# Index scores that trail their query tiles by two in a hybrid decoder step on one core

## Chip, cores and metric

One core of a Trainium2 chip runs the whole kernel. The metric is device time in microseconds (us) of one execution; the number given for a version is the median of its runs.

## What is computed

One inference step of a decoder layer, for a prompt of 256 tokens with 16 meta tokens ahead (272 rows) and for 8 samples with a paged cache of 1,024 tokens each (8 more rows, 280 in all). What matters here is how the attention picks its keys:

```python
proj = jnp.einsum('btd,dc->btc', _rmsnorm(x, g_mix_pre), w_in)
q, k, v, iq, ik, iw, u = jnp.split(proj, IN_OFFSETS, axis=-1)
s = jnp.einsum('bqhd,bsd->bqsh', iq, ik).astype(jnp.float32) * (IDX_DIM ** -0.5)
w = iw.astype(jnp.float32) * (N_IDX_HEADS ** -0.5)
scores = jnp.einsum('bqsh,bqh->bqs', jax.nn.relu(s), w)      # 16 index heads of width 64
_, idx = lax.top_k(jnp.where(admissible, scores, -jnp.inf), topk)
# attention over the chosen keys; pooling mixer on u; output projection; gated FFN with a short convolution
```

## The kernel before

Everything is float32, computed as three matmuls per product: a weight chunk is split into `hi` (ACT copies it, L415) and `lo` (DVE subtracts, L423), and PE multiplies hi by hi, hi by lo and lo by hi (L1409, L1410, L1412). A chunk is 128 x 1024 weights, 512 KB; SP loads it into one of four `raw` slots (L453) once the `lo` of the chunk four before is done. Two chunks make one tile of 128 output columns: 48 matmuls. The chunks are numbered in the order of the program: `C_IK` 0 and 1, `C_IQ` from 2 (eight index query tiles), `C_PROJ` from 18 (twenty tiles: eight of u, two each of k and v, eight of q), then the output projection `C_WOP`, `C_WOA`, the FFN.

Each engine has its program written out by hand, runs it in order and waits on semaphores. Around the change:

- PE: `q_idx_tile(0, t)` makes index query tile t, which holds index heads 2t and 2t+1; `weights_turned` (L1474) turns the heads' weights and lets DVE go on (`iw_ready`); `index_scores(h, p)` (L1470) multiplies the queries of heads h and h+1 with the index keys into banks 2 and 4. After the tiles come the scores of the last 16 queries (`iq3`, L1516), their weighted sum (L1521), then `proj_tile` by `proj_tile`, with the sample scores (L1540) after the first and their sum (L1548, waits for `sum3_used`) after the second.
- ACT: the `hi` of the chunks, the relu of each head's scores (`relu_head`, L668), and once, at the start, `root(1)` (L649, L652), the inverse root of the RMSNorm, with two loads of function tables.
- DVE: the `lo` of the chunks; `inv_rms(1)`; the index keys; `index_queries(t)` (seven instructions, the last is L896), which scales the queries of tile t; `index_sum(h)` (L954), which adds head h to the scores S; later, between projection tiles, nine `prompt_round` (top 8 of each row), `sample_lists`, `prompt_mask`, sixteen `sort_round` and `merge_lists`. In the attention loop over eight heads it does, for head h+1, `masked_scores` (L1177), then one piece of the sample's selection (`merge_quarters`, `compare_quarters`, `sample_threshold`, `sample_mask_1` to `3`), then the `lo` of a chunk, `head_low` (L1187) and the scaling of the probabilities (L1194, L1197), on which PE's transposes for the head wait (L1639).
- SP: between the weight loads it copies 64 cache pages, two DMAs each (`pages`, L464 to L466): three pages after an index tile's two chunks, then four, then two.

A head of the attention loop on PE is: transposes of the probabilities, scores of the next head (L1586), in heads 1, 2, 4 and 5 the `sample_scores` (L1597), the values (L1658 to L1660), one half tile of the output projection (24 matmuls).

## Time and profile before

| what | value |
|---|---|
| runs | 1218.87, 1219.74, 1219.9 us; median 1219.74 |
| the profiled execution | 1220.88 us, of which 1219.1 us are the span of the trace |
| PE busy | 1165.0 us (96%) |
| DVE busy | 816.8 us (67%) |
| ACT busy | 541.1 us (44%) |
| mean granted TensorE clock | 0.979 of full speed |
| DMA | 238.76 MB, mean 196 GB/s |

The trace has the start and duration of every instruction, and for an engine's idle time the event that ended it, in square brackets.
### The profile page before, as it was taken

The page shows a single profiled execution, that of the slowest core. Times are in us where ns is not written, and L with a number is a line of the kernel's source. Part 1 is how long each engine was busy: PE and PEld are TensorE (multiplying, and loading weights), DVE is VectorE, ACT ScalarE, POOL GpSimd, SP SyncE. Part 2 cuts the span into 40 slices and gives each one's busy share as a digit, 9 for nine tenths or more (in the row PEclk, how much of TensorE's full clock was granted, in tenths as well). Part 3 has the DMA queues.
Part 4 walks back from the last instruction along what each step waited for, and adds up shares of the span by engine and source line. Part 5 has one row for each costly group of instructions (what it writes and reads, how often), then busy time and mean ns, then how long its engine had stood idle before and what let it go on. Part 6 is the DMA issues. An engine that isn't in the chain of part 4 may idle for free.

```text
span 1219.1 us, 25889 instructions
## 1 busy us (share of the span) xinstructions
PE 1165.0 (96%) x9165; PEld 1120.7 (92%) x9165; DVE 816.8 (67%) x1543; ACT 541.1 (44%) x769; POOL 63.9 (5%) x70
## 2 busy tenths in 40 slices
PE   8989999999899899999999999999999899999992
PEld 7879999767698699999999999999999899999992
DVE  4775798776357977777777777777776444444444
ACT  7343333333235755445455544545454243333431
POOL 4700000000000400000000000000000000000002
PEclk9999999899899999999999999999999999999997
DMA  8878879655864365555555555555556666666641
GB/s 304 319 247 262 252 240 310 213 189 175 275 239 155 108 202 184 165 188 171 187 167 180 176 169 187 170 187 167 183 175 196 207 177 180 181 177 186 177 138 71
DMA packets 81080, 238.76 MB, mean 196 GB/s; under 512 B 9440, under 2 KB 28992, under 8 KB 78704
## 3 DMA queue, kind: packets, MB, share of 16 engines
q1 hardware_dynamic: 75152, 225.40, 57.9%
q10 hardware_dynamic: 4480, 9.01, 2.1%
q0 software_dynamic: 1408, 3.84, 0.9%
q8 instruction: 23, 0.38, 0.1%
q14 instruction: 17, 0.14, 0.0%
HBM read 231.64 MB, written 24.16 MB: 210 GB/s over the span
## 4 chain that ended last, share of the span: by engine, by line
PE 85%; DVE 6%; DMA 3%; SPq 3%; issue 1%; ACT 1%; DVEq 0%; POOL 0%; ACTq 0%; POOLq 0%
PE bank L1409 27%; PE bank L1410 27%; PE bank L1412 27%; DMA raw<-in_w_in 1%; DMA cache_ring<-vscr 1%; DVE part L1281 1%; DVE lo L423 1%; DMA x<-xscr 1%; PE bank L1586 1%; PE bank L1621 1%; SPq L466 1%; SPq L465 1%; SPq L464 0%; DVE h_lo L1286 0%; DVE short L1177 0%
## 5 line engine op out<-in xcount | busy, mean ns | idle before, releaser
L1409 PE MATMUL bank<-h_hi,hi 128*128 128x266 f32 (+1 forms) x2096 | 605.7, 289 | 1.5 <-DVE lo L423 1.5
L1412 PE MATMUL bank<-h_hi,lo 128*128 128x266 f32 (+1 forms) x2096 | 604.4, 288 | 0.0
L1410 PE MATMUL bank<-h_lo,hi 128*128 128x266 f32 (+1 forms) x2096 | 603.5, 288 | 0.0
L423 DVE TENSOR_TENSOR lo<-raw,hi 128x1024 fp32r<-128x1024 f32 (+2 forms) x362 | 431.5, 1199 | 212.9 <-ACT hi L415 189.9
L415 ACT ACTIVATE hi<-raw 128x1024 fp32r<-128x1024 f32 (+2 forms) x362 | 373.6, 1034 | 310.2 <-PE bank L1412 287.4
L1409 PEld LDWEIGHTS bank<-h_hi,hi 128*128 128x128 f32 x2096 | 399.0, 190 | 6.6 <-issue 4.4
L1410 PEld LDWEIGHTS bank<-h_lo,hi 128*128 128x128 f32 x2096 | 397.5, 190 | 0.1
L1412 PEld LDWEIGHTS bank<-h_hi,lo 128*128 128x128 f32 x2096 | 397.1, 189 | 0.0
L1409 PE MATMUL bank<-g_hi,hi 128*128 128x264 f32 x704 | 200.3, 285 | 5.0 <-DVE lo L423 5.0
L1410 PE MATMUL bank<-g_lo,hi 128*128 128x264 f32 x704 | 201.2, 286 | 0.0
L1412 PE MATMUL bank<-g_hi,lo 128*128 128x264 f32 x704 | 200.3, 284 | 0.0
L1409 PEld LDWEIGHTS bank<-g_hi,hi 128*128 128x128 f32 x704 | 133.4, 190 | 5.3 <-DVE lo L423 5.3
L1412 PEld LDWEIGHTS bank<-g_hi,lo 128*128 128x128 f32 x704 | 133.2, 189 | 0.0
L1410 PEld LDWEIGHTS bank<-g_lo,hi 128*128 128x128 f32 x704 | 132.8, 189 | 0.0
L1314 DVE SCALAR_TENSOR_TENSOR act<-up,par,act 128x256 f32<-128x256 f32 x176 | 84.9, 482 | 12.3 <-DVE act L1314 0.2
L807 ACT ACTIVATE g_hi<-act 128x264 f32 (+1 forms) x44 | 18.7, 425 | 143.4 <-DVE act L1328 143.4
L800 ACT ACTIVATE act<-up,par 128x264 f32<-128x264 f32 x88 | 53.5, 608 | 23.7 <-DVE up L1303 23.7
L432 POOL TENSOR_TENSOR o<-o,rms 128x528 f32<-128x528 f32 (+1 forms) x2 | 4.4, 2200 | 787.9 <-DVE rms L910 787.9
L821 ACT ACTIVATE act<-act 128x264 f32<-128x264 f32 x44 | 18.7, 425 | 50.3 <-DVE act L1317 50.3
L1330 DVE TENSOR_TENSOR g_lo<-act,g_hi 128x264 f32 (+1 forms) x44 | 19.1, 434 | 31.0 <-ACT g_hi L807 31.0
L1303 DVE TENSOR_TENSOR up<-bank,rms 128x266 f32<-128x266 f32 x88 | 37.6, 428 | 0.1
L599 POOL DMA_INDIRECT cache_ring<-in_cache_kidx,kix x32 | 34.0, 1064 | 23.2 <-DVE kix L875 13.8
(256 smaller groups left out, 651.0 us busy)
## 6 DMA issues: line engine op xcount, KB each, us to landing
raw<-in_w_up SPq DMA_DIRECT2D x176, 512.0 KB, 3.6
raw<-in_w_in SPq DMA_DIRECT2D x56, 512.0 KB, 5.2
raw<-in_w_down SPq DMA_DIRECT2D x64, 448.0 KB, 3.4
raw<-in_w_o SPq DMA_DIRECT2D x32, 512.0 KB, 4.5
raw<-in_w_down SPq DMA_DIRECT2D x32, 512.0 KB, 3.6
kscr<-in_cache_k SPq DMA_DIRECT2D x64, 128.0 KB
vscr<-in_cache_v SPq DMA_DIRECT2D x64, 128.0 KB
mixed<-kscr SPq DMA_DIRECT2D x8, 512.0 KB, 7.0
```

What stands on the lines that cost most here:

```text
L415: nc.scalar.activation(hi[:, s, 0:width], raw[:, s, 0:width], ACT.Copy).then_inc(hi_ready, 1)
L423: ops.tensor_tensor(lo[:, s, 0:width], raw[:, s, 0:width], hi[:, s, 0:width].bitcast(F32), ALU.subtract).then_inc(done, 1)
L599: nc.gpsimd.indirect_dma_start(kidx[:, b, g * PAGE:(g + 1) * PAGE], None, kidx_rows, bass.IndirectOffsetOnAxis(ap=kix[:, n:n + 1], axis=0) ...
L800: nc.scalar.activation(act[:, v, :], up[:, p, v, CONV - 1:], ACT.Identity, scale=par[:, bass.ds(CWT + 4 * FT + f, 1)], bias=par[:, bass.ds ...
L807: nc.scalar.activation(g_hi[:, bass.ds(r, 1), :], act[:, 0:1, :], ACT.Copy).then_inc(g_hi_ready, 1)
L821: nc.scalar.activation(act[:, 0, :], act[:, 0, :], ACT.Silu).then_inc(silu_ready, 1)
L1303: nc.vector.tensor_tensor(up[:, p, v, :], bank[(T_UP + v) % 2][:, L:T], rms[:, L:], mul).then_inc(up_ready, 1)
L1314: st.link(nc.vector.scalar_tensor_tensor(act[:, v, 0:SEQ], up[:, p, v, i:i + SEQ], par[:, bass.ds(CWT + 2 * FT * i + f, 1)], act[:, v, 0:S ...
L1330: nc.vector.tensor_tensor(g_lo[:, bass.ds(r, 1), :], act[:, 0:1, :], g_hi[:, bass.ds(r, 1), :].bitcast(F32), ALU.subtract).then_inc(g_lo_r ...
L1409: mm(out, w_hi, x_hi[:, k, first:], start=(opens and done == 0), stop=False)
L1410: mm(out, w_hi, x_lo[:, k, first:], start=False, stop=False)
L1412: last = mm(out, w_lo, x_hi[:, k, first:], start=False, stop=(closes and done == total))
```

## The change

Four index query tiles are kept instead of two (`iq`), and tile 3 gets a bank of its own. PE makes tiles 2 and 3 before `weights_turned` and the first scores; from there on the scores of tile t-2 follow tile t. Scores of the last heads (14) and of the last queries, the weighted sum and the sample scores move behind the projection tiles 0, 1 and 2. ACT and DVE split chunks `C_IQ + 6` and `C_IQ + 7` earlier, one of them ahead of `root(1)`; the relus and index sums lag accordingly. On DVE two rounds of the prompt's selection move into the q tiles, the sixteen sort rounds stand in the last three q tiles instead of four, and `merge_lists` and every later piece of the sample's selection move one place on, so that the attention loop starts with `merge_lists` and its head 6 has `sample_mask_3`.

```diff
@@ -244,7 +244,7 @@
-    iq = short[:, 0:2 * T].rearrange("p (h t) -> p h t", h=2)
+    iq = short[:, 0:4 * T].rearrange("p (h t) -> p h t", h=4)
@@ -288,7 +288,7 @@
-        return bank[3 if t == 2 else (T_IQ + t) % 2]
+        return bank[(3, 5)[t - 2] if t in (2, 3) else (T_IQ + t) % 2]
@@ -651,9 +651,10 @@
-            hi_chunk(ae, 0, C_IQ + 4)
-            hi_chunk(ae, 0, C_IQ + 5)
+            for j in range(4, 7):
+                hi_chunk(ae, 0, C_IQ + j)
...
+            hi_chunk(ae, 0, C_IQ + 7)
@@ -669,31 +670,25 @@
-            for t in (1, 2):
-                if t > 1:
-                    hi_chunk(ae, 0, C_IQ + 2 * t + 2)
-                    hi_chunk(ae, 0, C_IQ + 2 * t + 3)
-                for p in range(2):
-                    relu_head(2 * (t - 1) + p, p)
-            with ae.Fori(1, 3) as i:
-                for t in (1, 2):
-                    hi_chunk(ae, i, C_IQ + 2 * t + 2)
-                    hi_chunk(ae, i, C_IQ + 2 * t + 3)
-                    for p in range(2):
-                        relu_head(4 * i + 2 * (t - 1) + p, p)
-            hi_chunk(ae, 0, C_PROJ)
-            hi_chunk(ae, 0, C_PROJ + 1)
-            for h in range(12, 16):
+            def hi_tile(cj):
...
+                hi_chunk(ae, 0, cj)
+                hi_chunk(ae, 0, cj + 1)
...
+            for t in range(4, 9):
+                hi_tile(C_IQ + 2 * t)
+                for n in range(0 if t == 4 else 2 * t - 8, 2 * t - 6):
+                    relu_head(n, n % 2)
+            for h in range(10, 14):
...
-                if h < 14:
-                    hi_chunk(ae, 0, C_PROJ + h - 10)
-                if h == 13:
-                    ae.wait_ge(score3_done, 1)
-                    for n in range(2):
-                        nc.scalar.activation(relu3[n], bank[3 + 2 * n][:, 0:TP], ACT.Relu,
-                                             scale=IDX_SCALE).then_inc(relu3_ready, 1)
-            hi_chunk(ae, 0, C_PROJ + 4)
-            hi_chunk(ae, 0, C_PROJ + 5)
+            hi_tile(C_PROJ + 2)
+            for h in range(14, 16):
+                relu_head(h, h % 2)
+            ae.wait_ge(score3_done, 1)
+            for n in range(2):
+                nc.scalar.activation(relu3[n], bank[3 + 2 * n][:, 0:TP], ACT.Relu,
+                                     scale=IDX_SCALE).then_inc(relu3_ready, 1)
+            hi_tile(C_PROJ + 4)
@@ -881,8 +876,8 @@
-                if t >= 2:
-                    dve.wait_ge(iq_used, 2 * t - 2)
+                if t >= 4:
+                    dve.wait_ge(iq_used, 2 * t - 6)
@@ -893,7 +888,7 @@
-                nc.vector.tensor_tensor(iq[:, t % 2, L:], ps[:, L:T], rms[:, L:], mul).then_inc(iq_ready, 1)
+                nc.vector.tensor_tensor(iq[:, t % 4, L:], ps[:, L:T], rms[:, L:], mul).then_inc(iq_ready, 1)
@@ -920,7 +915,9 @@
+            lo_chunk(dve, nc.vector, lo_dve, 0, C_IQ + 6)
...
+            lo_chunk(dve, nc.vector, lo_dve, 0, C_IQ + 7)
@@ -961,23 +958,20 @@
-                if t in range(2, 8):
+                if t >= 3:
...
-                if t >= 2:
-                    index_sum(2 * t - 4)
-                    index_sum(2 * t - 3)
+                    index_sum(2 * t - 6)
+                    index_sum(2 * t - 5)
...
-            for h in range(12, 16):
-                index_sum(h)
-                if h == 13:
-                    lo_chunk(dve, nc.vector, lo_dve, 0, C_PROJ + 2)
-                    lo_chunk(dve, nc.vector, lo_dve, 0, C_PROJ + 3)
-            dve.wait_ge(sum3_done, 1)
-            acc = S[0:16, S_AT[2]:S_AT[2] + TP]
-            nc.vector.tensor_tensor(acc, acc, misc[0:16, 128:128 + TP], ALU.add).then_inc(sum3_used, 1)
-            dve.wait_ge(sum3_used, 1)
...
+            def index_sum_3():
...
+                dve.wait_ge(sum3_done, 1)
+                acc = S[0:16, S_AT[2]:S_AT[2] + TP]
+                nc.vector.tensor_tensor(acc, acc, misc[0:16, 128:128 + TP], ALU.add).then_inc(sum3_used, 1)
+                dve.wait_ge(sum3_used, 1)
@@ -1075,11 +1069,18 @@
                     lo_chunk(dve, nc.vector, lo_dve, 0, C_PROJ + 2 * t + j)
 
             for t in range(U0, U0 + 8):
-                if t:
-                    low_halves(t + 1)
+                if t == 0:
+                    index_sum(10)
+                    index_sum(11)
+                low_halves(t + 1)
+                if t < 2:
+                    index_sum(2 * t + 12)
+                    index_sum(2 * t + 13)
                 if t == 2:
+                    index_sum_3()
+                if t == 3:
                     sample_lists()
-                else:
+                elif t >= 2:
                     prompt_round(next(rounds_p))
                 ps = tile_ready(t)
                 nc.vector.tensor_tensor(U[:, t, POOL_BUF:POOL_BUF + T], ps[:, 0:T], rms[:, :],
@@ -1131,15 +1132,13 @@
                 h = t - Q0
                 if h < HEADS - 1:
                     low_halves(t + 1)
-                if h < 2:
+                if h < 4:
                     prompt_round(next(rounds_p))
-                if h == 2:
+                if h == 4:
                     prompt_mask()
-                if h in range(3, 7):
-                    for n in range(4 * h - 12, 4 * h - 8):
+                if h >= 5:
+                    for n in range(((0, 5, 10, 16))[h - 5], ((0, 5, 10, 16))[h - 4]):
                         sort_round(n)
-                if h == 7:
-                    merge_lists()
                 ps = tile_ready(t)
                 g = h // (HEADS // KV)
                 off = 32 * g + h
@@ -1200,17 +1199,19 @@
                 if h + 1 < HEADS:
                     masked_scores(h + 1)
                     if h == 0:
+                        merge_lists()
+                    if h == 1:
                         merge_quarters()
                         compare_quarters(0, 4)
-                    if h == 1:
+                    if h == 2:
                         compare_quarters(4, 8)
-                    if h == 2:
+                    if h == 3:
                         sample_threshold()
-                    if h == 3:
+                    if h == 4:
                         sample_mask_1()
-                    if h == 4:
+                    if h == 5:
                         sample_mask_2()
-                    if h == 5:
+                    if h == 6:
                         sample_mask_3()
                     lo_chunk(dve, nc.vector, lo_dve, 0, C_WOP + 4 + h)
                     head_low(h)
@@ -1459,15 +1460,16 @@
-            def index_scores(h, p):
...
-                if not isinstance(h, int) or h >= 2:
+            def index_scores(h):
...
+                pe.wait_ge(iq_ready, h // 2 + 1)
+                if h >= 2:
...
-                        last = mm(o, iq[rows, p, q0:q0 + nq], ikT[rows, 0:nk], start=True, stop=True)
+                        last = mm(o, iq[rows, h // 2 % 4, q0:q0 + nq], ikT[rows, 0:nk], start=True, stop=True)
@@ -1500,26 +1495,15 @@
+            q_idx_tile(0, 3)
...
-            for t in range(2):
-                pe.wait_ge(iq_ready, t + 1)
-                index_scores(2 * t, t)
-            with pe.Fori(1, 3) as i:
-                q_idx_pair(i, i)
-            pe.wait_ge(iq_ready, 6)
-            q_idx_tile(0, 7)
-            pe.wait_ge(iq_ready, 7)
-            index_scores(12, 0)
...
-            pe.wait_ge(iq_ready, 8)
-            for n in range(2):
-                last = mm(bank[3 + 2 * n][:, 0:TP], iq3[:, P * n:P * n + P], ikT[0:IDX_DIM, 0:TP], start=True, stop=True)
-            last.then_inc(score3_done, 1)
-            index_scores(14, 1)
-            pe.wait_ge(relu3_ready, 2)
-            for n in range(2):
-                last = mm(misc[0:16, 128:128 + TP], iwq3[:, n, :], relu3[n], start=(n == 0), stop=(n == 1))
-            last.then_inc(sum3_done, 1)
+            index_scores(0)
+            index_scores(2)
+            for t in range(4, 8):
+                pe.wait_ge(iq_ready, t - 3 if t < 6 else t - 1)
+                q_idx_tile(0, t)
+                index_scores(2 * t - 4)
+            index_scores(12)
@@ -1530,6 +1514,15 @@
+            index_scores(14)
+            for n in range(2):
+                last = mm(bank[3 + 2 * n][:, 0:TP], iq3[:, P * n:P * n + P], ikT[0:IDX_DIM, 0:TP], start=True, stop=True)
+            last.then_inc(score3_done, 1)
+            proj_tile(0, 1, T_PROJ + 1)
+            pe.wait_ge(relu3_ready, 2)
+            for n in range(2):
+                last = mm(misc[0:16, 128:128 + TP], iwq3[:, n, :], relu3[n], start=(n == 0), stop=(n == 1))
+            last.then_inc(sum3_done, 1)
@@ -1540,14 +1533,15 @@
-            proj_tile(0, 1, T_PROJ + 1)
+            proj_tile(0, 2, T_PROJ + 2)
...
-            with pe.Fori(0, 5) as i:
+            proj_tile(0, 3, T_PROJ + 3)
+            with pe.Fori(1, 5) as i:
```

On ACT, at the start of the program (`rms` is the inverse root, `hi` a chunk's high half), before and after:

```order
L415 ACTIVATE hi<-raw 128x1024 [waits chunk_used,raw_loaded2]
L415 ACTIVATE hi<-raw 128x1024 [waits chunk_used,raw_loaded3]
L649 ACT_TABLE_LOAD
L649 ACTIVATE rms<-bank,con 128x280 [waits sum_ready]
L652 ACT_TABLE_LOAD
L652 ACTIVATE rms<-rms 128x280 [waits ln_ready]
L658 DMA part<-in_pool_w 128x2048 [waits h_lo_ready]
L659 DMA part<-in_state_pool 128x960
L668 ACTIVATE short<-bank 128x384 [waits iq_used] x2
```

```order
L415 ACTIVATE hi<-raw 128x1024 [waits chunk_used,raw_loaded2]
L415 ACTIVATE hi<-raw 128x1024 [waits chunk_used,raw_loaded3]
L415 ACTIVATE hi<-raw 128x1024 [waits chunk_used,raw_loaded0]
L649 ACT_TABLE_LOAD
L649 ACTIVATE rms<-bank,con 128x280 [waits sum_ready]
L652 ACT_TABLE_LOAD
L652 ACTIVATE rms<-rms 128x280 [waits ln_ready]
L415 ACTIVATE hi<-raw 128x1024 [waits chunk_used,raw_loaded1]
L659 DMA part<-in_pool_w 128x2048 [waits h_lo_ready]
L660 DMA part<-in_state_pool 128x960
L415 ACTIVATE hi<-raw 128x1024 [waits chunk_used,raw_loaded2]
L415 ACTIVATE hi<-raw 128x1024 [waits chunk_used,raw_loaded3]
```

The high half of `C_IQ + 6` now stands ahead of the table loads, with its wait for the chunk's DMA, and three more high halves ahead of the first relus.

On DVE, after the weights of the index heads are there (`iwq`, `iwz`; L886 to L891 are one `index_queries`), the order is now:

```order
L939 COPY iwq<-bank 128x32 [waits iw_ready,iq_ready]
L941 TENSOR_TENSOR iwq<-bank,con 128x16 x2
L943 TENSOR_TENSOR iwz<-bank,con 128x8
L886 TENSOR_TENSOR short<-bank,rms 64x4 [waits chunk_used,s_loaded,dve_step]
...
L891 TENSOR_TENSOR short<-bank,rms 128x266
L886 TENSOR_TENSOR short<-bank,rms 64x4 [waits chunk_used,iq_ready]
...
L891 TENSOR_TENSOR short<-bank,rms 128x266
L423 TENSOR_TENSOR lo<-raw,hi 128x1024 [waits chunk_used,hi_ready,iq_ready]
L423 TENSOR_TENSOR lo<-raw,hi 128x1024 [waits chunk_used,hi_ready]
```

Before, one `index_queries` stood between `iwq` and the first `lo` (that of `C_IQ + 6`); now two stand there, and the first `lo` is that of `C_IQ + 8`.

On DVE, in head 6 of the attention loop (L1176 and L1180 are the end of `masked_scores`, L1196 the scaling that PE waits for):

```order
L1180 TENSOR_SCALAR nmx<-mx 128x2 [waits dve_step]
L1181 TENSOR_SCALAR nmx<-mx 16x1
L1056 SCALAR_TENSOR_TENSOR short<-Ss,thr,short 8x1025
L1057 TENSOR_TENSOR Ws<-Ws,short 8x1025 [waits dve_step]
L1058 TENSOR_SCALAR Ws<-Ws 8x1025 [waits dve_step]
L423 TENSOR_TENSOR lo<-raw,hi 128x1024 [waits chunk_used,hi_ready]
L1186 TENSOR_TENSOR h_lo<-bank,h_hi 128x258 [waits o_hi]
L1193 RECIPROCAL rden<-den 128x3 [waits exp_done]
L1196 TENSOR_SCALAR short<-short,rden 128x128 [waits dve_step]
```

Before, head 6 had nothing between its `masked_scores` and the `lo`; these three instructions of `sample_mask_3` stood in head 5.

## Rows read from the trace of the kernel before

**Rows 1.** Stretches of the index stage and the projections: busy time by engine, clock, DMA

```profile
core 0: us, PE busy (x) PEld busy (x) DVE busy (x) ACT busy (x) POOL busy (x), PEclk, DMA share, GB/s
27.40:32.60 5.20, 5.20 (x42) 5.11 (x42) 2.81 (x3) 5.15 (x6) 4.18 (x4) 1.00 0.92 278
39.65:44.68 5.03, 2.74 (x25) 1.92 (x25) 3.13 (x13) 2.76 (x4) 3.97 (x4) 1.00 1.03 407
44.68:52.33 7.65, 7.65 (x49) 7.50 (x49) 7.32 (x18) 2.88 (x4) 6.02 (x6) 0.78 0.83 275
52.33:59.31 6.98, 6.98 (x57) 6.50 (x56) 5.72 (x15) 2.77 (x4) 5.26 (x6) 1.00 0.78 249
80.27:88.88 8.61, 5.20 (x26) 2.21 (x25) 6.34 (x17) 4.21 (x8) 0.00 (x0) 0.83 0.71 235
88.88:96.97 8.09, 8.09 (x49) 7.93 (x48) 3.63 (x13) 1.06 (x1) 0.00 (x0) 0.76 0.72 232
96.97:113.50 16.53, 16.53 (x140) 15.16 (x140) 9.49 (x27) 5.38 (x7) 0.00 (x0) 1.00 0.77 242
107.24:217.35 110.11, 110.11 (x872) 110.03 (x873) 91.41 (x242) 37.15 (x38) 0.00 (x0) 1.00 0.84 271
```

**Rows 2.** Timeline of PE: the small products of the index stage

```profile
52.33 0.93 PE L1470 MATMUL bank<-ikT,short 64*128 64x128 f32 x8
82.75 1.18 PE L1516 MATMUL bank<-ikT,short 64*128 64x272 f32 x4 [1.56 <-DVE short L896]
86.89 1.99 PE L1521 MATMUL bank<-short,iwq 128*16 128x272 f32 x4 [0.41 <-ACT short L693]
```

**Rows 3.** Timeline of DVE behind the turned weights

```profile
40.71 0.19 DVE L942 COPY iwq<-bank 128x32 f32<-128x32 f32 x1 [2.11 <-PE bank L1482]
41.17 0.35 DVE L891 TENSOR_TENSOR short<-bank,rms 64x4 f32<-64x4 f32 x2
42.35 0.43 DVE L896 TENSOR_TENSOR short<-bank,rms 128x266 f32<-128x266 f32 x1
43.40 2.36 DVE L423 TENSOR_TENSOR lo<-raw,hi 128x1024 fp32r<-128x1024 f32 x2 [0.61 <-DVE short L896]
```

**Rows 4.** Weight loads of chunks C_IQ + 6 and + 7, from issue to landing

```profile
L453 SPq DMA_DIRECT2D raw<-in_w_in x2: 430/501/572, 27.4 to 28.0; - x2
...
DMA to landing us min/median/max: 5.2/5.2/5.2
```

**Rows 5.** Timeline of ACT, the inverse root

```profile
29.58 1.28 ACT L649 ACT_TABLE_LOAD   x1
30.88 0.49 ACT L649 ACTIVATE rms<-bank,con 128x280 f32<-128x280 f32 x1
32.69 0.44 ACT L652 ACTIVATE rms<-rms 128x280 f32<-128x280 f32 x1
```

**Rows 6.** Timeline of SP's queue, the loads of query tile 6 and projection tile 3

```profile
53.96 0.94 SPq L453 DMA_DIRECT2D raw<-in_w_in  x2
...
97.90 0.95 SPq L453 DMA_DIRECT2D raw<-in_w_in  x2
```

**Rows 7.** Heads 0, 1, 3, 4, 5, 6 of attention, transposes to transposes (columns of rows 1)

```profile
230.95:240.88 9.93, 9.83 (x43) 7.54 (x43) 6.94 (x27) 3.27 (x11) 0.00 (x0) 0.66 0.27 99
240.88:249.22 8.34, 8.34 (x58) 5.78 (x59) 5.94 (x23) 3.48 (x10) 0.00 (x0) 1.00 0.23 71
257.54:266.36 8.82, 6.75 (x44) 5.18 (x43) 6.65 (x19) 4.32 (x11) 0.00 (x0) 1.00 0.92 296
266.36:277.03 10.67, 10.03 (x58) 6.42 (x59) 7.04 (x18) 2.98 (x10) 0.00 (x0) 0.84 0.78 246
277.03:286.37 9.34, 8.51 (x59) 5.74 (x59) 7.10 (x19) 3.69 (x11) 0.00 (x0) 1.00 0.17 59
286.37:293.33 6.96, 6.80 (x42) 5.23 (x43) 4.09 (x16) 2.70 (x11) 0.00 (x0) 1.00 0.32 96
```

**Rows 8.** DVE from start to end of each selection piece: merge_lists, merge_quarters, threshold, masks 1 to 3

```profile
212.29:216.67 4.38, 4.10 (x17) 1.00 1.01 332
235.13:238.33 3.20, 2.96 (x11) 0.50 0.00 0
252.84:254.73 1.89, 1.69 (x8) 1.00 0.00 0
261.14:263.82 2.68, 2.61 (x6) 1.00 1.10 361
271.40:274.49 3.09, 3.02 (x5) 1.00 0.98 332
280.69:283.85 3.16, 3.09 (x6) 1.00 0.00 0
```

More of the change, by code:

```diff
@@ L1482, in weights_turned @@
                 mm(misc[:, 64:72], con[0:16, HREP:HREP + P], iwT[:, TP:T], start=True, stop=True).then_inc(iw_ready, 1)
-            def q_idx_pair(r, n):
-                for t in (1, 2):
-                    pe.wait_ge(iq_ready, 2 * n + t - 1)
-                    q_idx_tile(r, t)
-                    pe.wait_ge(iq_ready, 2 * n + t)
-                    index_scores(4 * n + 2 * (t - 1), (t - 1) % 2)
             ident = con[:, IDN:IDN + P]
```

## The prediction

> **What bounds the kernel now.** I read the busy times first, then a table of stretches with the granted clock, then PE's timeline with the event that ended each pause. PE is busy 96% of the span and DVE 67%, so only time that PE loses, or spends at its lower clock, counts. From 107.24 to 217.35 us PE is busy for 110.11 of 110.11 us at clock 1.00, that is 2.4 GHz: nothing can be won there [rows 1]. It loses time in three places.
>
> The first is the pause before index tile 3: in 5.03 us PE works 2.74, so 2.29 are lost, and the tile behind it takes 7.65 at a mean clock of 0.78 [rows 1]. The next stretch, one tile and one product of scores, takes 6.98 at clock 1.00; without the scores (0.93, [rows 2]) a tile is 6.05, so the fall of the clock cost 1.6. The second is the end of the index stage: 8.61 us with 5.20 busy, so 3.41 lost, and the projection tile behind it takes 8.09 at clock 0.76 [rows 1], against about 6.2 at full clock (16.53 us hold two tiles and the sample's products): 1.9. PE's last product there stretched to 1.99, at half clock [rows 2]. The third is attention, where the intervals are longer than PE's busy time in heads 0, 3, 4 and 5 [rows 7].
>
> **The index stage, to the start of projection tile 3.** Before, it starts at 113.50 [rows 1]. After, tile 2 still ends at about 39.65 and tile 3 follows at once, so to 45.7, if its weights are there. Its chunks land at 27.4 + 5.2 = 32.6 and little later [rows 4]. The high half of C_IQ + 6 now stands ahead of root(1) on ACT and waits for that landing: root(1), which began at 29.58 and took 3.55 to 33.13 [rows 5], begins near 33.6 and moves 4 us back, to about 37.2. The index keys and queries 0 behind it on DVE, and the split of C_IQ + 7, then end near 40 to 42; PE needs the split inside tile 3, at about 42.7 (half of the tile), and the queries at 46. So I cost the move at nothing; its cover is tile 3, and 1 us more would eat most of it.
>
> Then the weights are turned. From the end of tile 2 (39.65, [rows 1]) to DVE's copy of them took 1.06, to 40.71; from there to the end of queries 1 it took 2.07, to 42.78 [rows 3]. After: copy at 46.8, queries 1 at 48.8. PE does scores 0 meanwhile and is done at 47.6, so it idles 1.2; scores 2 end at 49.8. But now a second set of queries (1.6, from 41.17 to 42.78) stands on DVE ahead of the first low half that tile 4 needs (1.2; two took 2.36): 48.8 + 1.6 + 1.2 = 51.6 [rows 3]. PE idles 1.8 more. **The first pause is not removed; it moves behind tile 3 and becomes 3.0 instead of 2.29.** With the same fall of the clock behind it (1.6), tile 4 ends at 51.6 + 6.05 + 1.6 = 59.3. Before, it ended at 59.31, with one product of scores more done.
>
> From there on: scores 4 (0.93), tiles 5 to 7 with scores (3 x 6.98 = 20.95), about 1.0 of waiting for two relus of ACT before scores 12 (one wait of that kind took 0.41, [rows 2]; two relus on ACT are more; between 0.4 and 2), scores 12 (0.93), three projection tiles with the sample's products (16.53 + 6.2 = 22.73, [rows 1]), scores 14 (0.93), the last queries (1.18, [rows 2]) and their weighted sum (1.99 at half clock, so 1.0): 49.65. Tile 3 of the projection starts at 109.0 instead of 113.50: **4.5 us gained**. The waits of the second pause now lie beside projection tiles.
>
> SP is the next to be late. It may load a chunk once the low half of the chunk four before is done. The loads of tile 6 wait for the low half of C_IQ + 9, at 52.8, so they leave 1.1 earlier than 53.96 [rows 6], and since SP's queue is full of page copies behind them, so do later loads: those of projection tile 3 at 96.8 instead of 97.90 [rows 6], while PE is 4.5 ahead. Landing takes 5.2 [rows 4], the two high halves and the last low half about 3, the sum of the last queries, which stands behind them on DVE and on which PE's sample sum waits, about 0.5: 105.7. PE gets there at 109.0 less half of the 4.1 that the sample's two products take (16.53 - 2 x 6.2), about 106.9. About 1.2 us of slack: hidden, but a gain over 5.7 is cut off here.
>
> **The projections.** A moved index sum, prompt round or sort round delays PE only if DVE falls behind by more than the two banks allow. DVE is busy 91.41 of 110.11 us [rows 1], and the last three query tiles get five or six sort rounds instead of four. Cost nothing; the cover is that DVE's slack.
>
> **Attention.** A head's interval is the longer of PE's own path and DVE's, on which PE's transposes wait. DVE's path is a fixed part plus that head's selection piece: head 3 has 8.82 with a piece of 2.68, so 6.14 fixed [rows 7, 8]; head 5, 9.34 - 3.16 = 6.18, agrees. PE's own path is 8.34 with sample scores (heads 1, 2, 4, 5) and about 6.8 without (head 6, 6.80 busy) [rows 7]. Each piece moves one head on, and merge_lists (4.38, [rows 8]), which was hidden under a projection tile, joins head 0:
>
> - head 0: 9.93 - 3.20 + 4.38 = 11.11
> - head 1: 6.14 + 3.20 = 9.34 (was 8.34)
> - head 2: 8.34; its piece fitted into 8.34 in head 1
> - head 3: 6.14 + 1.89 = 8.03 (was 8.82)
> - head 4: 6.14 + 2.68 = 8.82 (was 10.67)
> - head 5: 6.14 + 3.09 = 9.23 (was 9.34)
> - head 6: 6.14 + 3.16 = 9.30 (was 6.96)
>
> That is 64.17 against 62.38 (286.37 + 6.96 - 230.95): 1.8 lost. In it head 4's 10.67 is gone: by the rule it was 9.23, and 1.44 came from half clock after the 2.07 of idle in head 3 (8.82 - 6.75) [rows 7]. After, that pause shrinks to 1.3, but head 6 idles 9.30 - 6.80 = 2.5, and I price the fall behind it at the same 1.44: **3.2 us lost**. Masks 2 and 3, which fell into heads with 8.34 of PE work, now fall partly into heads without.
>
> **Sum.** -4.5 + 3.2 = -1.3: the profiled execution goes from 1220.88 to 1219.5. It lies 1.14 above the median of 1219.74, so the median becomes 1218.4. Bounds: index stage -5.7 (SP's limit) to -2.6 (one more fall of 1.9), attention +1.8 to +6 (three falls): from -3.9 to +3.4.
>
> **The rivals.** *Faster:* the clock recovers inside the pause of tile 4, which PE's short products at 47 and 49 break in two, so tile 4 runs at full speed; the index stage then gains up to SP's limit, 5.7, and if head 6's pause costs no fall either, attention loses 1.8: -3.9, 1215.8. For it: the two idle pieces are 1.2 and 1.8, each shorter than head 3's 2.07, after which the clock fell. Against: the pause of 2.29 before tile 3 was broken by small products as well, and tile 3 ran at 0.78. *Slower:* falls also follow the new short pauses, before scores 12 (1.9) and in heads 1 and 3 (2 x 1.44): -1.3 + 4.8 = +3.5, 1223.2. It decides as soon as a pause of 1.0 to 1.3 is enough. Against it: 0.83 of idle in head 5 and 0.64 in head 4 left the following heads at 1.00 [rows 7]; for it: nothing between 0.83 and 2.07 is shown. *Late weights:* the DMA engines are 0.71 to 0.83 busy through the index stage [rows 1]; if landing takes 8 instead of 5.2, because the loads come closer to other transfers, the last-query sum is at 108.6, PE waits 1.7 and the time is +0.4, 1220.1. It decides from about 6.4. The Trainium skill ("DMA: Bandwidth & Descriptors", Issuing engines are not separate DMA queues) states that DMAs of all issuing engines run on the same 16 DMA engines and interleave; by that rule an earlier issue by SP need not land earlier, which speaks for this rival. In the trace the 5.2 of C_IQ + 6 was reached with the engines 0.92 busy from 27.40 to 32.60 [rows 1, 4], which speaks against it. *The change doesn't do what it says* is partly my forecast already: the tiles ahead of the scores do not remove the first pause.
>
> **How the numbers follow.** The forecast has 0.44, the faster rival 0.32, the slower one 0.12, late weights 0.07, the rest 0.05, half on each side. 0.2% is 2.4 us, about what a measurement can tell from no change; so faster means under 1217.3, slower over 1222.2. The forecast's own spread (the wait before scores 12, 0.4 to 2; one fall more or less) takes it from 1217 to 1220, a sixth of it below 1217.3. Faster: 0.32 + 0.06 + 0.02 = 0.40; slower: 0.12 + 0.02 = 0.14; the same: 0.46. The range goes from 1214.6, a little below the faster rival, to 1222.6, within the slower one.
>
> **What would show it.** Right: PE runs 0 to 45.7 without the pause at 40, idles about 3.0 between 46.6 and 51.6, tile 4 shows a clock below 0.9; no 3.4 of idle between 80 and 90; projection tile 3 starts at 109 and PE is full from there; heads 0 to 6 take 11.1, 9.3, 8.3, 8.0, 8.8, 9.2 and 9.3, with one stretch of half clock after head 6. Wrong: tile 3 waits for C_IQ + 7's low half (root(1) was moved into the path), PE waits at the sample sum, projection tiles wait for DVE, or a clock below 1.00 where I have none.

## The result and the profile after

The changed kernel takes 1222.41 us (median of 20 runs, 1221.19 to 1224.69), the kernel before, run on the same chips, 1219.82 (20 runs, 1216.62 to 1222.23). The ratio is 1.0024, with an interval of 1.0017 to 1.0031: **2.6 us slower** by the medians, where 1.4 faster was forecast. The profiled execution took 1224.69, the longest of the 20, with a span of 1222.9 and a mean clock of 0.974; so it shows where time can go, and a second profile (below) shows what of it comes back.

Table of stretches of the changed kernel (columns as in [rows 1]): the two pauses of the index stage, the projections, then heads 0, 1, 4, 6, and head 7 up to its last product with the values.

```profile
45.70:52.14 6.44, 3.18 (x25) 2.02 (x25) 4.65 (x20) 2.92 (x5) 5.06 (x5) 0.80 1.02 404
52.14:59.85 7.71, 7.71 (x47) 7.71 (x48) 7.38 (x18) 3.06 (x4) 5.94 (x6) 0.73 0.81 264
81.90:90.20 8.30, 7.25 (x58) 6.78 (x56) 6.08 (x14) 3.75 (x6) 0.00 (x0) 1.00 0.62 190
90.20:109.10 18.90, 18.90 (x152) 16.50 (x152) 10.20 (x22) 7.67 (x13) 0.00 (x0) 1.00 0.82 263
105.00:213.40 108.40, 108.40 (x863) 108.17 (x862) 91.24 (x241) 37.12 (x38) 0.00 (x0) 1.00 0.83 269
227.65:238.35 10.70, 6.78 (x43) 5.21 (x43) 8.12 (x33) 4.33 (x11) 0.00 (x0) 0.95 0.24 87
238.35:249.53 11.18, 11.07 (x59) 6.68 (x59) 7.04 (x27) 2.44 (x10) 0.00 (x0) 0.74 0.16 51
265.94:276.00 10.06, 10.05 (x58) 6.40 (x59) 6.61 (x18) 2.43 (x9) 0.00 (x0) 0.83 0.89 286
285.24:294.58 9.34, 6.81 (x42) 5.24 (x42) 7.09 (x19) 3.75 (x11) 0.00 (x0) 1.00 0.19 55
...
294.58:306.56 11.98, 11.98 (x45) 9.29 (x45) 4.08 (x12) 2.28 (x8) 0.00 (x0) 0.57 1.02 341
```

PE's timeline of the changed kernel, the rows with waits that matter:

```profile
49.15 1.32 PE L1472 MATMUL bank<-ikT,short 64*128 64x128 f32 x8 [1.59 <-DVE short L891]
52.14 0.56 PE L1410 MATMUL bank<-h_hi,hi 128*128 128x266 f32 x1 [1.67 <-DVE lo L423]
83.01 0.93 PE L1472 MATMUL bank<-ikT,short 64*128 64x128 f32 x8 [1.05 <-ACT short L669]
238.35 0.88 PE L1633 MATMUL bank<-con,short 114*128 114x114 f32 x3 [3.91 <-DVE short L1196]
294.58 0.59 PE L1633 MATMUL bank<-con,short 114*128 114x114 f32 x3 [2.53 <-DVE short L1196]
334.10 0.64 PE L1615 MATMUL bank<-mixed,probsT 128*32 128x256 f32 x2 [3.26 <-DMA cache_ring<-vscr]
```

The index stage went as forecast: tile 3 without a pause, then 1.59 + 1.67 us of idle behind it (3.0 forecast), a fall of the clock to 0.73 over tile 4, 1.05 before scores 12, no other wait. The sample sum ends at 109.5 (109.0 forecast), and PE is full from there. Attention is where the forecast breaks: head 1 runs at 0.74 behind 3.91 us of idle, head 4 at 0.83 behind 1.30, head 7 at 0.57 behind 2.53. The last row of the timeline is a wait for the sample's value pages, 3.26 here. PE's timeline of the kernel before has 5.55 for it in the first profile and 3.26 in the second:

```profile
332.06 0.64 PE L1621 MATMUL bank<-mixed,probsT 128*32 128x256 f32 x2 [5.55 <-DMA cache_ring<-vscr]
```

```profile
329.71 0.64 PE L1621 MATMUL bank<-mixed,probsT 128*32 128x256 f32 x2 [3.26 <-DMA cache_ring<-vscr]
```

So it varies between executions of one kernel (3.3 to 5.6 over all profiles), and it takes up nothing of the loss. From the end of head 7's stretch the rest of the span takes 915.5 to 916.9 us in all fourteen profiles behind this document (1222.9 - 306.56 = 916.3 here), whatever came before. Several expectations below count on the wait to take back a part; it does not.

DVE in the changed kernel behind the turned weights, against [rows 3]:

```profile
46.81 0.19 DVE L939 COPY iwq<-bank 128x32 f32<-128x32 f32 x1 [3.22 <-PE bank L1484]
...
48.66 0.43 DVE L891 TENSOR_TENSOR short<-bank,rms 128x266 f32<-128x266 f32 x1
...
50.30 0.43 DVE L891 TENSOR_TENSOR short<-bank,rms 128x266 f32<-128x266 f32 x1
50.77 2.36 DVE L423 TENSOR_TENSOR lo<-raw,hi 128x1024 fp32r<-128x1024 f32 x2
```

DVE idled 3.22 us for the turned weights with two sets of queries still to make, ends queries 1 and 2 at 49.1 and 50.7, and only then splits the chunks of tile 4.

### The profile page after: what moved, and what is told of

Read it like the earlier page. It is cut to its first block, busy times and chain, and to the rows that moved or that the text cites. A ratio compares the mean times of both kernels' runs of the same rounds, so it can differ in the third digit from the quotient of the medians.

```text
span 1222.9 us, 25853 instructions
## 1 busy us (share of the span) xinstructions
PE 1168.5 (96%) x9165; PEld 1122.9 (92%) x9165; DVE 816.9 (67%) x1543; ACT 540.8 (44%) x769; POOL 65.2 (5%) x70
## 4 chain that ended last, share of the span: by engine, by line
PE 83%; DVE 9%; DMA 3%; SPq 2%; issue 1%; ACT 1%; DVEq 0%; POOL 0%; ACTq 0%; POOLq 0%
PE bank L1410 26%; PE bank L1411 26%; PE bank L1413 26%; DVE lo L423 2%; DMA raw<-in_w_in 2%; DMA cache_ring<-vscr 1%; DVE part L1282 1%; DMA x<-xscr 1%; PE bank L1580 1%; PE bank L1615 1%; DVE h_lo L1287 0%; PE bank L1591 0%; DVE o L1389 0%; DVE o L432 0%; DVE short L1004 0%
```

## The experiments

All are variants of the changed kernel unless said otherwise. "Sample sum" is the time at which PE's `ssum` product ends; in the kernels with the changed index stage a projection tile more (6.2 us) lies ahead of it. For comparison that tile is taken off.

**The whole selection early.** Does the shift of the selection lose what the index stage wins?

```diff
@@ tiles of u
+                for n in range(*{3: (0, 2), 4: (2, 3), 5: (3, 4), 6: (4, 5), 7: (5, 6)}.get(t, (0, 0))):
+                    sort_round(n)
@@ query tiles
-                if h >= 5:
-                    for n in range(((0, 5, 10, 16))[h - 5], ((0, 5, 10, 16))[h - 4]):
-                        sort_round(n)
+                for n in range(*{1: (6, 7), 2: (7, 8), 3: (8, 9), 5: (9, 13), 6: (13, 16)}.get(h, (0, 0))):
+                    sort_round(n)
+                if h == 7:
+                    merge_lists()
@@ attention: the pieces of heads 0 to 5 as in the kernel before
```

> The changed kernel with the sample's selection as early as before the change: nine of the sixteen sort rounds stand beside the projection tiles of u and the first query tiles, where DVE idled about 1 us a tile, merge_lists is back in the last query tile, and heads 0 to 5 have the pieces they had before. Theory (the later selection is what loses, by PE pauses of 4.3, 1.3 and 2.5 us in heads 0, 3 and 6 and the half clock behind them): projection tile 3 starts near 109.5 as in the changed kernel, the heads take the 62.4 us of before, and the index stage's 4.0 us are kept: 1215.8, up to 1217 if the wait for the copied value pages (5.55 us before) takes a part. Rival (the index stage's gain is taken back at the next transfer, whatever attention does): 1219.8.

Measured: 1219.23 (12 runs, 1215.44 to 1221.27), ratio to before 0.9998 (0.9987 to 1.0009). So the changed kernel's loss is gone, but nothing is won over the kernel before: in the number the rival is nearer, and the theory's 1215.8 was reached only by the quickest of the twelve executions (1215.44), which is the profiled one. The rival's reason fails all the same: from the sample sum to the first transposes of head 0 every profile with the changed index stage takes 117.4 to 118.1 us, and behind head 7 nothing is taken back (above). (The pause of head 0 is 3.9 in the profile, not the 4.3 of the expectation.) That asked for a second profile (at the end of this section).

**The shift alone**, in the kernel before:

```diff
-                if h in range(3, 7):
-                    for n in range(4 * h - 12, 4 * h - 8):
+                if h >= 5:
+                    for n in range(((0, 5, 10, 16))[h - 5], ((0, 5, 10, 16))[h - 4]):
                         sort_round(n)
-                if h == 7:
-                    merge_lists()
...
                     if h == 0:
+                        merge_lists()
+                    if h == 1:
                         merge_quarters()
```

(and each later piece one head on; the rounds of the prompt's selection stay).

> The kernel before, with the sort rounds in the last three query tiles, merge_lists in head 0 and each later piece one head on, index stage untouched. Theory (pauses and falls of the clock): heads 0 to 6 take about 67 instead of 62.4, head 7 about 11 instead of 8.1, so up to 8 us by then, of which the wait for the value pages takes 2 to 4: 1224 to 1226. Rival (only the path on DVE counts, 1.8 us, and the falls were chance): 1220 to 1221.6.

Measured: 1224.25, ratio 1.0040 (1.0025 to 1.0055): the shift costs **4.9 us** by itself. Its heads 1 and 7, in the table of stretches:

```profile
239.09:250.51 11.42, 11.42 (x58) 6.75 (x59) 7.04 (x26) 2.44 (x9) 0.00 (x0) 0.70 0.15 54
294.36:304.80 10.44, 10.44 (x44) 8.41 (x44) 4.07 (x12) 2.28 (x8) 0.00 (x0) 0.67 1.04 343
```

Both run at a lowered clock behind the pauses of heads 0 and 6, without any change in the index stage. By the ratios (1.0040 and 1.0024) the changed kernel is 2.0 us better than this one, which is then what the index stage wins, give or take 2 by the intervals. Its own index stage, which is that of the kernel before, ended the sample sum at 104.70, where the first profile of before has 107.24.

**Queries 1 and 2 first.** Is the pause behind tile 3 the order of DVE's work?

```diff
             index_queries(0)
+            index_queries(1)
+            index_queries(2)
+            lo_chunk(dve, nc.vector, lo_dve, 0, C_IQ + 8)
             dve.wait_ge(iw_ready, 1)
...
-                    lo_chunk(dve, nc.vector, lo_dve, 0, C_IQ + 2 * t + 2)
+                    if t > 3:
+                        lo_chunk(dve, nc.vector, lo_dve, 0, C_IQ + 2 * t + 2)
...
-                if t:
-                    index_queries(t)
+                    index_queries(t)
```

> The changed kernel with index queries 1 and 2 and the low half of chunk C_IQ + 8 ahead of the turned weights on DVE, where it idled 3.2 us. Theory (the pause behind tile 3 is DVE's order, not data): the 3.26 us of idle between 46 and 52 fall under 1, tile 4 runs at full clock, projection tile 3 starts near 105: 1217.8 (4.6 less than the changed kernel). Rival (weights: the loads of chunks C_IQ + 8 to + 11 took 6 to 11 us to land, so PE waits for them instead): 1220.5 to 1222.4.

Measured: 1219.32, ratio 1.0001 (0.9986 to 1.0016), 3.1 under the changed kernel. The sample sum ends at 107.1, not near 105: the wait for low halves is gone, but a new one stands before scores 2, in PE's timeline:

```profile
49.17 1.65 PE L1475 MATMUL bank<-ikT,short 64*128 64x128 f32 x8 [1.74 <-ACT short L669]
```

The relus of heads 0 and 1 stand on ACT behind the high half of C_IQ + 9, on which ACT began at 47.2 after a wait of 2.25 for the chunk to land. So DVE's order was half of the pause and a landing on ACT's path the next one.

**The changed kernel again**, no edit.

> The changed kernel once more, for a second profile. Theory (falls belong to the pauses in heads 0, 3 and 6): heads 1, 4 and 7 again take about 11.2, 10.1 and 11.2 us at a mean clock under 0.9, the others their path times within 0.2. Rival (chance): at least one of the three runs at 1.00.

Measured: 1222.74. Stretches of tile 4 and of heads 1, 4 and 7:

```profile
52.07:59.90 7.83, 7.83 (x43) 7.83 (x44) 7.50 (x18) 2.90 (x4) 6.00 (x7) 0.64 0.83 276
238.37:249.84 11.47, 11.47 (x59) 6.64 (x60) 7.04 (x26) 2.44 (x9) 0.00 (x0) 0.70 0.20 67
266.19:275.06 8.87, 8.52 (x58) 5.97 (x59) 6.62 (x19) 2.69 (x10) 0.00 (x0) 1.00 0.92 297
293.68:305.40 11.72, 11.72 (x44) 8.78 (x44) 4.06 (x12) 2.28 (x8) 0.00 (x0) 0.58 1.04 336
```

The falls in heads 1 and 7, behind 3.91 and 2.53 us of idle, are there again; that in head 4, behind 1.30, is not, so the rival as it was worded came true. The long pauses have a fall behind them in both profiles, the short one in one of the two.

**PE kept at work in the pauses.** The path on DVE stays, the idle time goes:

```diff
                 if h:
                     w_o_tile(h)
+                fill = {0: 7, 1: 25, 4: 8, 7: 16}.get(h, 0)
+                if fill:
+                    pe.wait_ge(tile_freed, 21 + h)
+                for _ in range(fill):
+                    mm(bank[(T_WOP + h + 1) % 2][:, 0:352], idle[:, 0:P], idle[:, 0:352], start=True, stop=True)
                 pe.wait_ge(prob_ready, 3 * h + 3)
```

> The changed kernel with matmuls on zeros (352 columns, into the bank of the next half tile of the output projection) ahead of PE's wait for the probabilities in heads 0, 1, 4 and 7 (7, 25, 8 and 16 of them, 1.0, 3.5, 1.1 and 2.2 us at full clock, all within the pauses). The path on DVE is unchanged. Theory (the clock falls behind idle PE): heads 0, 3 and 6 stay at 10.7, 8.05 and 9.34, heads 1 and 4 go to 9.3 and 8.8, head 7 (to the last product with the values) from 10.4 to 12 down to about 7.5: 5 to 7 us by then, of which the wait for the value pages takes about half: 1218.5 to 1220. Rival (the falls have another cause than the idle time): 1222.4 as the changed kernel.

Measured: 1218.84, ratio to before 0.9992 (0.9983 to 1.0001), 3.6 under the changed kernel. Heads 0, 1, 4 and 7:

```profile
226.28:237.01 10.73, 10.73 (x69) 9.20 (x68) 8.22 (x33) 4.33 (x11) 0.00 (x0) 1.00 0.29 98
237.01:246.51 9.50, 8.51 (x59) 5.74 (x59) 7.05 (x27) 3.33 (x10) 0.00 (x0) 1.00 0.17 60
262.92:271.80 8.88, 8.52 (x58) 5.75 (x59) 6.63 (x19) 2.69 (x10) 0.00 (x0) 1.00 0.95 300
290.42:299.26 8.84, 8.84 (x45) 7.28 (x44) 4.07 (x12) 2.28 (x8) 0.00 (x0) 0.81 1.00 319
```

Head 0 is as long as without fills, since its path is DVE's; heads 1 and 4 run at 1.00, head 7 is 3.1 us shorter. For head 1 the idle time is shown as the cause: behind 3.91 of it the clock was at 0.70 to 0.74 in all three profiles without fills. For head 4 this run says little, since head 4 ran at 1.00 without fills too. The rival falls. The median is in the expected range, but not for its reason: in the profiles head 7 ends 6.1 to 7.3 us earlier than in the changed kernel and the span is 5.7 to 7.7 shorter, so no later wait took half. The median gains less because this profiled execution was the quickest of its eleven (1217.01).

From the first transposes of head 0 to those of head 7 it takes 64.14 us, and 64.17 was forecast for the path without falls. Head 7 still falls a little, here and in both profiles of the kernel before, where its pause is 0.16 long; the first of them:

```profile
293.33:302.22 8.89, 8.89 (x44) 7.33 (x45) 4.17 (x12) 3.28 (x9) 0.00 (x0) 0.81 1.04 353
```

So a pause right ahead of it is not the only thing that a fall in head 7 comes with. What else it is was not tried.

**Only merge_lists early**: the sort rounds as in the first experiment, and

```diff
                 if h == 7:
+                    merge_lists()
...
-                    if h == 0:
-                        merge_lists()
                     if h == 1:
```

> The changed kernel with merge_lists back in the last query tile (nine sort rounds moved ahead as in the run with the whole selection early); the pieces of heads 1 to 6 stay one head late. Theory (head 0's pause of 3.9 us and the fall behind it are the dearest part): head 0 goes from 10.7 to about 7, head 1 from 11.3 to 9.3, together 5.5, of which later waits take up to half: 1217 to 1219.5. Rival (head 6's pause ahead of head 7 is the dear part): 1221 to 1222.

Measured: 1219.53, ratio to before 1.0002 (0.9994 to 1.0011), 2.9 under the changed kernel. Heads 0, 1 and 7:

```profile
228.07:236.82 8.75, 6.78 (x43) 5.21 (x43) 4.00 (x16) 4.32 (x11) 0.00 (x0) 1.00 0.32 120
236.82:246.32 9.50, 8.52 (x58) 5.74 (x58) 7.05 (x27) 3.32 (x10) 0.00 (x0) 1.00 0.20 59
290.21:302.14 11.93, 11.93 (x44) 8.98 (x45) 4.07 (x12) 2.28 (x8) 0.00 (x0) 0.57 1.02 337
```

Head 0 falls to 8.75, not 7: without a piece DVE waits 2.51 for the high half of its chunk, which ACT makes after the exponentials of the head, as DVE's timeline shows:

```profile
234.27 1.23 DVE L423 TENSOR_TENSOR lo<-raw,hi 128x1024 fp32r<-128x1024 f32 x1 [2.51 <-ACT hi L415]
```

Head 1 has no fall behind a pause of 1.97. That is 3.6 for the two heads; head 7 keeps its 11.9. The median lies at the upper edge of the theory's range and under the rival's. So merge_lists in head 0 is the dearest part, and head 6's pause costs beside it.

**Selection early, queries first, relus ahead**: the first and the third experiment together, and on ACT

```diff
+                if t == 4:
+                    hi_chunk(ae, 0, C_IQ + 8)
+                    relu_head(0, 0)
+                    relu_head(1, 1)
+                    hi_chunk(ae, 0, C_IQ + 9)
+                    continue
                 hi_tile(C_IQ + 2 * t)
```

> The run with the whole selection early and the run with queries 1 and 2 first in one kernel, and on ACT the relus of heads 0 and 1 ahead of the high half of chunk C_IQ + 9, on whose landing they stood. Theory (the losses add up, and no other wait comes in): no pause over 0.5 us between 46 and 52 and none of half clock behind it, the sample sum ends near 105.5 where the changed kernel has 109.5 to 110.1, heads as before the change: 1214.5 to 1216. Rival (the earlier index stage meets late weights): PE waits for chunks C_IQ + 10 to + 13 and the time stays at 1218 to 1219.

Measured: 1214.70, ratio to before **0.9959** (0.9947 to 0.9972). Behind the turned weights (compare the first two rows of the profile after):

```profile
45.70:49.70 4.00, 2.95 (x27) 2.11 (x26) 3.09 (x14) 1.81 (x3) 3.19 (x3) 1.00 1.03 401
49.70:56.00 6.30, 6.30 (x54) 6.15 (x56) 6.01 (x14) 3.46 (x5) 5.28 (x4) 1.00 1.01 371
```

1.05 us of idle are left of 3.26 (under 0.5 was expected), tile 4 runs at full clock, and PE does not wait for later weights. The sample sum ends at 106.35, 0.85 later than expected (two waits for relus, 0.65 and 1.61, near 78). The gain holds to the end.

**The kernel before again**, no edit.

> The kernel before once more, for a second profile. Theory (the second pause of the index stage was long in the first profile because chunk C_PROJ + 1 landed late, at 83.9, and the fall of the clock was of chance length): the wait before scores 14 is not 1.44 again, and the sample sum ends at 104.5 to 106 instead of 107.24, so the changed index stage saves 1 to 2.5 us and not 4. Rival (the first profile is typical): 107.2 within 0.3.

Measured: 1220.14. The sample sum ends at 105.93, 1.3 earlier. Scores 14 stand behind the high half of a chunk on ACT (it is C_PROJ + 2, not + 1 as the expectation has it), which waits for the chunk to land. ACT's timeline in the first profile of before, in this one, and in the run with the shift alone, which has the same index stage:

```profile
83.88 1.06 ACT L415 ACTIVATE hi<-raw 128x1024 fp32r<-128x1024 f32 x1 [2.17 <-DMA raw<-in_w_in]
```

```profile
84.29 1.06 ACT L415 ACTIVATE hi<-raw 128x1024 fp32r<-128x1024 f32 x1 [2.41 <-DMA raw<-in_w_in]
```

```profile
82.43 1.06 ACT L415 ACTIVATE hi<-raw 128x1024 fp32r<-128x1024 f32 x1 [0.79 <-DMA raw<-in_w_in]
```

So the wait before scores 14 was the same in the second profile (1.37 for 1.44): that half of the theory fails there, and holds for the third execution, which has none. What differs between the first two is the clock. Projection tile 0 of this run:

```profile
89.28:95.66 6.38, 6.38 (x49) 6.22 (x48) 3.65 (x13) 1.06 (x1) 0.00 (x0) 1.00 0.84 277
```

6.38 at 1.00, against 8.09 at 0.76 in [rows 1]. Both executions ran their pause at a lowered clock (0.83 and 0.80); in the first the tile behind it did so too.

Attention differs as well. In the first profile head 0 ran at 0.66 and took 9.93 [rows 7]; here it runs at 1.00 and takes 9.48, and head 1, behind a pause of 2.69, falls:

```profile
239.11:250.58 11.47, 11.47 (x59) 6.64 (x59) 6.01 (x23) 2.44 (x9) 0.00 (x0) 0.70 0.26 88
```

A like fall of the clock cost 0.45 in head 0, which waits for DVE in any case, and 3.1 in head 1 (11.47 against 8.34 [rows 7]), where PE sets the pace.

**Fills in three kernels.** Matmuls on zeros as above, 7, 17, 12, 4 and 4 of them in heads 0, 1, 4, 5 and 6, to take the falls' chance out of the comparison: in the kernel before, in the one with the selection early, and in the one with all three edits.

> The kernel before with matmuls on zeros (352 columns each) ahead of PE's wait for the probabilities in heads 0, 1, 4, 5 and 6 (7, 17, 12, 4 and 4 of them, all within the pauses of 1.2, 2.7, 2.1, 0.8 and 0.8 us). Both theories expect falls of the clock in heads 0, 1 and 4 to go, 1 to 3 us off: 1217 to 1219. It is the base for the next run.

> The same matmuls on zeros in the run with the whole selection early, that is the changed index stage with the selection of before. Theory (the changed index stage is worth the 2 to 2.5 us by which its sample sum ends earlier in the profiles, and the falls in attention hid it in the medians): 2 to 2.5 below the run of the kernel before with the same fills. Rival (a later wait, that for the value pages, takes the gain back): within 0.7 of it.

> The same matmuls on zeros in the run with the selection early, queries 1 and 2 first and the relus ahead. If both hold that the index stage counts and that the falls in heads 0, 1 and 4 cost: 1 to 3 us under its 1214.7, so 1211.5 to 1213.5. If later waits take it: 1214 to 1215.

Measured: 1216.22 (ratio to before 0.9978, 0.9966 to 0.9989), 1214.77 (0.9965, 0.9952 to 0.9978) and 1212.15 (0.9948, 0.9935 to 0.9961). The first is 3.2 better than before, more than expected; the second 1.45 better than the first, between what theory and rival expected, and the intervals overlap; the third is **the best of the study**, 7.3 under the kernel before, and some 10 under the changed one. Head 7 of the first ran without a fall, that of the second did not:

```profile
290.17:297.53 7.36, 7.36 (x44) 5.80 (x44) 4.05 (x10) 3.13 (x9) 0.00 (x0) 1.00 1.00 324
```

```profile
288.02:296.91 8.89, 8.89 (x44) 7.27 (x44) 4.29 (x12) 3.28 (x9) 0.00 (x0) 0.81 1.04 352
```

In the profiles the second starts head 7 2.15 us earlier, which is what the theory asks for, and loses 1.53 of it to that fall. The wait for the value pages is 3.77 and 3.57: the rival's reason does not hold.

**The selection early, again**, no edit to the first experiment's kernel.

> The run with the whole selection early once more, for a second profile, since its first was its quickest of twelve executions. Theory (chance falls in attention make up the scatter): the sample sum again ends at 103 to 104 plus a tile (109 to 110.2), and heads 0 to 7 together take 2 to 4 us more than in the first. Rival (the index stage itself scatters): it ends later than 110.5.

Measured: 1219.74. Head 7 in the first profile of that kernel, and in this one:

```profile
290.13:297.51 7.38, 7.38 (x45) 5.82 (x45) 4.06 (x10) 3.13 (x9) 0.00 (x0) 1.00 1.03 341
```

```profile
290.57:300.99 10.42, 10.42 (x44) 8.56 (x45) 4.16 (x12) 3.28 (x9) 0.00 (x0) 0.67 1.03 343
```

The sample sum ends at 110.1 (109.4 in the first), heads 0 to 6 take 62.9 (63.2), and head 7 alone takes 3.0 more. 4.3 us lie between two executions of one kernel, and 3.0 of them are one fall of the clock.

## Why the prediction was wrong

**The shape was right, two sizes were not.** In the prediction's own terms the forecast was -4.5 in the index stage and +3.2 in attention. The +3.2 is a longer path (64.17 against 62.38 less the fall of 1.44 in head 4) and nothing for the falls of the clock, one of 1.44 before and one after. The profiles give about -2.4 in the index stage, +3.5 for the path and +2.2 for the falls.

*The index stage, -4.5: mis-sized.* The changed side came out nearly as worked out (109.5 for 109.0; the mean over seven profiles with that index stage is 109.8). The side of before was wrong. The step that failed is the row 88.88:96.97 [rows 1] taken as the stage's price: "the projection tile behind it takes 8.09 at clock 0.76". In the other three profiles with the old index stage that tile took 6.38, 6.99 and 7.35. The sample sum ended at 107.24, 105.93, 104.70 and 105.96 in the four, mean 106.0; with a tile taken off, the changed stage has 109.8 - 6.2 = 103.6. That is 2.4 saved, not 4.5. The medians with equal attention give less: 2.0 (changed kernel against the shift alone, give or take 2), 1.45 with fills (as wide), and 0.0 (selection early against before, interval about 1.3 each way). Since nothing behind the sample sum takes the gain back in a profile, the falls in attention are what could hide it; whether they do in the executions without a profile stays open. The first profile was the unlucky one. The hint was there: its execution was 1.14 above the median, and the prediction took that off both sides ("so the median becomes 1218.4"), though part of it sat in just the pause that the change removes.

*Attention's path: right within 0.3.* The rule (6.14 plus the piece, PE's 8.34 where that is longer) gave 64.17, and 64.14 was measured once the falls are filled. That close a match is luck: head 0 was put 0.4 too high, because its 9.93 [rows 7] holds half clock (0.66) and 9.48 is its length without, and heads 1 to 6 were put 0.3 too low in all. The fills in the kernel before make its own path 60.60 (229.57 to 290.17), so the path costs 3.5, where the sum had 3.2.

*The falls, one of 1.44 on either side: the step that failed in attention.* In the sum "head 1: 6.14 + 3.20 = 9.34" stands at full clock, though head 0 ahead of it now idles 3.9: head 1 took 11.18, 11.47 and 11.42 in the three profiles with that order, 1.7 to 2.0 more than the 9.50 with fills. Head 7 behind head 6's pause was priced at 1.44 more; it took 11.98, 11.72 and 10.44, against 7.36 without a fall and 8.89 in both profiles of before: 1.5 to 3.1 more than before. Head 4 fell in one of two profiles of the changed kernel. Counted against the fills, the falls over heads 0 to 7 take 3.3 and 4.6 us in the kernel before and 7.4, 6.2 and 4.9 with the shift, 2.2 more in the mean.

By the profiles that is -2.4 + 3.5 + 2.2 = +3.3, and the two profiled executions of each kernel lie 3.2 apart in the mean; the medians of twenty lie 2.6 apart. With the medians of the experiments in place of the profiles (0.0 to 2.0 for the index stage, 4.9 for the shift) the sum is +2.9 to +4.9. So the account is good to about 2 us, no better.

*The rivals.* The faster one failed on its condition: tile 4 ran at 0.73 and 0.64, not at full speed. The slower one had the mechanism, a fall behind new pauses, but named the short ones (scores 12, heads 1 and 3). Of those the 1.05 before scores 12 cost nothing (clock 1.00 after it), head 3's cost 1.2 in some executions, and the dearest pause, head 0's 3.9, stood in no rival, though the list of heads gave its size: 11.11 less 6.8. Against it the prediction said that no pause between 0.83 and 2.07 is shown; the trace has one of 1.18 ahead of head 0, whose own row shows 0.66 [rows 7]. Late weights did not happen: no wait for a low half after tile 4, and the stage's loads kept up even when PE was 3.4 earlier (106.35 for 109.8). The Trainium skill ("DMA: Bandwidth & Descriptors", Issuing engines are not separate DMA queues) states that transfers of all issuing engines interleave on the same DMA engines. No run here isolates that; the rows show only that an earlier issue need not land earlier: SP issued the load of the chunk C_PROJ + 2 above at 78.75, 78.52 and 77.93 in the three executions, and it landed at 83.9, 84.3 and 82.4. "Root(1) moved at no cost" held: no wait in tile 3.

*On the clock.* What shows cause is the runs with fills: the same path, idle time replaced by work, falls gone. In the four profiles with fills no head from 0 to 6 has a fall; of the ten without, nine have one or more. The Trainium skill ("TensorE: Matmul & The Clock Gate", HAM oscillation — how this bites in real kernels) describes a matmul loop in which PE waits for data ahead of each stretch of work and each stretch starts at the lower clock. The rows without fills agree for the long pauses: a fall stands behind 3.91 in three of three, behind 2.69 in four of four, behind 2.53 in five of five. Behind 2.07 it is four of five, behind 1.30 two of five, behind the 1.2 ahead of head 0 two of nine. Head 7 is not explained by its pause alone: behind 0.15 to 0.17 it fell in five of eight profiles.

## What to carry to other kernels

A pause of PE has two prices, its own length and the slower work behind it; the second is chance in size and depends on whether PE sets the pace where it falls, so take it from several profiles, and when the profiled execution is off the median, find in which stage before moving that difference to the other side. Work that a change pushes out of a covered place (here merge_lists, 4.4 us under a projection tile) has to be priced where it lands, and so does each pause that it makes for the clock behind it. Where a pause can't be removed, matmuls on zeros that fit into it are worth trying: they gave 3.2 us in the kernel before, without touching its order.

## What was not expected of the hardware

The time of head 7, from its first transposes to its last product with the values, lies near four values in all fourteen profiles: 7.4, 8.9, 10.4 and 11.7 to 12.0. The same kernel gave 7.38 in one execution and 10.42 in the next. A change that moves the time by less than such a step (1.5 us) can't be read from the whole time of one profile of each kernel.
